# A mixture-of-experts layer whose gathered token blocks are transposed on VectorE instead of TensorE

## What is computed

```python
def swiglu(t, wg, wu, wd):
    return (jax.nn.silu(t @ wg) * (t @ wu)) @ wd

def moe_ffn(h, ...):                       # h: 512 x 1024
    scores = jax.nn.sigmoid(t @ w_router)  # 64 experts, group-limited top 8
    ...
    wts = wts / jnp.sum(wts, axis=-1, keepdims=True) * ROUTED_SCALE
    ...
    def expert_block(args):
        tok, wb, e = args
        xb = t_pad[tok]                    # gather the rows of this block
        yb = swiglu(xb, w_e_gate[e], w_e_up[e], w_e_down[e])
        return yb * wb[:, None]
    ...
    routed = jax.ops.segment_sum(yb.reshape(P, d), slot_tok, num_segments=T + 1)[:T]
    shared = swiglu(t, w_sh_gate, w_sh_up, w_sh_down)
    return routed + shared
```

## Time and profile before

| What | us |
|---|---|
| Median of three runs (lowest, highest) | 1122.77 (1122.42, 1122.96) |
| The profiled execution, whole | 1125.14 |
| Its span in the trace | 1123.3 |
| First gate_up of the loop starts | 402.82 |
| Last gate_up of the loop starts | 1083.4 |
| TensorE busy (share of the span) | 1030.9 (92%) |
| VectorE busy | 442.9 (39%) |
| ScalarE busy | 437.9 (39%) |
| GpSimd busy | 371.0 (33%) |

### The profile page before, as it was taken

How to read it: one execution, slowest core, us unless ns; L and a number is a source line. 1 busy time by engine, 2 the same in 40 slices (tenths; PEclk the granted TensorE clock), 3 DMA queues, 4 the chain that set the end, 5 groups by cost and what they waited for, 6 DMA issues and landing times.

```text
span 1123.3 us, 20142 instructions
## 1 busy us (share of the span) xinstructions
PE 1030.9 (92%) x6035; PEld 543.3 (48%) x6036; DVE 442.9 (39%) x727; ACT 437.9 (39%) x929; POOL 371.0 (33%) x242
## 2 busy tenths in 40 slices
PE   1899999899999999899999799999999999999980
PEld 0554443566455644455455355455555554554540
DVE  0445776874478522222232223232232232322325
ACT  3312122575343534334444334444444434444442
POOL 1112233000000044344444335454444444444440
PEclk9999999999999999999999999999999999999995
DMA  9933255700007389999759999999988986999915
GB/s 311 391 138 143 92 207 183 295 1 1 19 38 280 137 318 387 402 385 374 226 163 343 402 390 388 297 388 335 398 283 256 350 312 199 369 386 361 321 14 224
DMA packets 76169, 295.10 MB, mean 263 GB/s; under 512 B 16657, under 2 KB 17169, under 8 KB 56433
## 3 DMA queue, kind: packets, MB, share of 16 engines
q1 hardware_dynamic: 50386, 258.01, 58.2%
q0 software_dynamic: 24336, 34.29, 13.8%
q10 hardware_dynamic: 1424, 2.52, 0.6%
HBM read 280.83 MB, written 36.44 MB: 282 GB/s over the span
## 4 chain that ended last, share of the span: by engine, by line
PE 71%; DMA 13%; DVE 6%; issue 3%; ACT 3%; POOL 2%; SPq 1%; DVEq 0%; ACTq 0%; POOLq 0%
PE psum L1104 32%; PE psum L1113 16%; PE psum L1091 5%; DMA wring<-in_w_e_down 4%; DMA ring<-in_w_ada 4%; DMA heads<-in_w_ada 3%; PE psum L912 2%; PE psum L1120 2%; PE psum L1063 2%; PE psum L934 2%; PE psum L880 2%; PE psum L963 2%; PE psum L943 2%; POOL ring L488 2%; DVE heads L1242 1%
## 5 line engine op out<-in xcount | busy, mean ns | idle before, releaser
L1104 PE MATMUL psum<-wring,rows 128*64 x1664 | 387.2, 386 | 15.5 <-issue 14.3
L1104 PE MATMUL psum<-cur_g,rows 128*64 128x256 f32 x1664 | 387.5, 387 | 0.0
L1104 PEld LDWEIGHTS psum<-wring,rows 128*64 128x64 f32 x1664 | 222.0, 138 | 136.4 <-issue 31.5
L504 POOL DMA_INDIRECT expert_sums<-rows,sidx x107 | 203.9, 1906 | 96.0 <-issue 73.7
L1104 PEld LDWEIGHTS psum<-cur_g,rows 128*64 128x64 f32 x1664 | 222.0, 138 | 0.0
L498 POOL DMA_INDIRECT xg<-h_rows,gidx x107 | 114.0, 1065 | 291.4 <-ACT gidx L739 281.8
L1113 PE MATMUL psum<-wring,rows 128*64 x420 | 202.7, 605 | 1.6 <-issue 1.6
L1113 PE MATMUL psum<-cur_d,rows 128*64 128x512 f32 x420 | 202.7, 605 | 0.0
L1504 DVE COPY cur_g<-wring 128x2048 f32 x105 | 128.8, 1227 | 127.2 <-issue 86.2
L736 ACT COPY cur_d<-wring 128x1024 f32 x105 | 109.8, 1046 | 29.2 <-issue 29.2
L800 ACT COPY rows<-psum 128x512 f32<-128x512 f32 x105 | 61.5, 585 | 133.0 <-PE psum L1113 125.8
(11 more groups left out here) (223 smaller groups left out, 998.4 us busy)
## 6 DMA issues: line engine op xcount, KB each, us to landing
wring<-in_w_e_gate SPq DMA_DIRECT2D x64, 1024.0 KB
wring<-in_w_e_up SPq DMA_DIRECT2D x64, 1024.0 KB
wring<-in_w_e_down SPq DMA_DIRECT2D x64, 1024.0 KB
ring<-in_w_ada SPq DMA_DIRECT2D x16, 1024.0 KB, 4.8
ring<-in_w_in SPq DMA_DIRECT2D x4, 2048.0 KB, 29.8
ring<-in_w_ada SPq DMA_DIRECT2D x2, 2048.0 KB, 24.8
heads<-in_w_ada SPq DMA_DIRECT2D x2, 2048.0 KB, 33.4
ring<-in_w_out SPq DMA_DIRECT2D x1, 4096.0 KB, 16.4
```

Source lines behind the costliest of these rows:

```text
L504: pool.indirect_dma_start(srows[q], bass.IndirectOffsetOnAxis(sidx[:, q:q + 1].bitcast(U32), 0), ysb[:, q, :], None, bounds_check=2 * T - ...
L1104: last = pe.matmul(pp[2][SUB * g:SUB * g + SUB, 512 * q:512 * q + 2 * P] .rearrange("p (u f) -> p u f", u=2), xT[:, q, k % 4, c0:c0 + SUB] ...
```

## The change

`h` is stored in its natural order, and `gather` fetches quarters: partition 32*c + r of `xg` gets the 256 features of quarter c of the tokens in slots r (first half of the free dimension) and 32 + r (second half). That takes two indirect DMAs a block, of 128 rows of 1 KB each, where there was one of 128 rows of 2 KB. Since a quarter is what 32 partitions of the weights hold (eight features each), transposing each 32x32 piece within its 32 partitions gives `xT`. VectorE does this in one operation (`turn_block` in its own list, behind `copy_gate_up` and ahead of `hmid`), with a read stride of eight floats. TensorE's `turn_block` and ScalarE's `evacuate_block` are gone. `gather_index` copies two columns and waits until VectorE has turned the block whose buffer it frees.

The indices need each slot's token on four groups of partitions. TensorE gets eight small matmuls for it (`quarters`) in the middle of the last shared gate_up, between VectorE's copy of the raw table and VectorE's operations that make the indices. `expert_input` reads without a stride; `turn_h` takes every eighth column instead.

The core of the diff:

```diff
             def gather(b, q, set_by):
                 pool.wait_ge(s_gi, set_by)
                 pool.sem_inc(s_pgo, 1)
-                pool.indirect_dma_start(xg[:, q, :], None, hrows, bass.IndirectOffsetOnAxis(gidx[:, q:q + 1].bitcast(U32), 0),
-                                        bounds_check=2 * T - 1, oob_is_err=False).then_inc(s_gt[q], 16)
+                for s in range(2):
+                    pool.indirect_dma_start(xg[:, q, 256 * s:256 * s + 256], None, hrows,
+                                            bass.IndirectOffsetOnAxis(gidx[:, q, s:s + 1].bitcast(U32), 0),
+                                            bounds_check=4 * T - 1, oob_is_err=False).then_inc(s_gt[q], 16)
...
-            def evacuate_block(n, q):
-                act.wait_ge(s_xt, n)
-                act.copy(xT[:, q], pp[1][:, 512 * q:512 * q + 512].rearrange("p (k s) -> p k s", k=4)).then_inc(s_xte, 1)
...
             def gather_index(b, q):
-                act.copy(gidx[:, q:q + 1], slot_idx[:, bass.ds(b + 1, 1)]).then_inc(s_gi, 1)
+                act.wait_ge(s_xte, b - 1)
+                act.copy(gidx[:, q, :], slot_g[:, bass.ds((b + 1) * 2, 2)]).then_inc(s_gi, 1)
...
                 for k in range(KD):
-                    last = pe.transpose(pp[3][:, k * P:(k + 1) * P], y1[:, t % 2, k * P:(k + 1) * P], ident)
+                    last = pe.transpose(pp[3][:, k * P:(k + 1) * P],
+                                        y1[:, t % 2, k:D:KD], ident)
...
+            def quarters():
+                pe.wait_ge(s_raw, 1)
+                for s in range(2):
+                    for c in range(4):
+                        last = pe.matmul(pp[2][32 * c:32 * c + 32, MAXB * s:MAXB * s + MAXB],
+                                         cst[:, C_ID + 32 * s:C_ID + 32 * s + 32], vraw, start=True, stop=True)
+                last.then_inc(s_sel2, 1)
...
-                    c0 = SUB * (k // 4)
...
-                                         xT[:, q, k % 4, c0:c0 + SUB], cur_g[:, q, :, k, :] if g else w[:, :, k, 0:P],
+                                         xT[:, q, k, :], cur_g[:, q, :, k, :] if g else w[:, :, k, 0:P],
...
-            shared_gate_up(3, range(4, KD))
+            shared_gate_up(3, range(4, 6))
+            quarters()
+            shared_gate_up(3, range(6, KD))
             shared_down(2)
             shared_hidden(3)
+            shared_down(3)
             pe.wait_ge(s_clr, 2)
-            pe.wait_ge(s_gt[0], 16)
-            turn_block(0)
-            shared_down(3)
...
                     gate_up(q, w0)
-                    pe.wait_ge(s_gt[1 - q], i * 8 + 16 * (q + 1))
-                    turn_block(1 - q)
...
+            def turn_block(q, gathered):
+                dve.wait_ge(s_gt[q], gathered)
+                dve.transpose(xT[:, q].rearrange("p k (s r) -> p s k r", s=2),
+                              xg[:, q, :].rearrange("p (s r k) -> p s k r", s=2, k=KD)).then_inc(s_xte, 1)
...
                     copy_gate_up(i + (q + 1), 1 - q)
+                    turn_block(1 - q, i * 16 + 32 * (q + 1))
                     dve.wait_ge(s_sil, i + (q + NT + 1))
```

More of the change, by code:

```diff
@@ L68 @@
 C_EPS = C_FAC + 64
-NCONST = C_EPS + 1
+C_QUART = C_EPS + 1
+NCONST = C_QUART + 1
 def constants():
@@ L100, in constants @@
     c[:, C_EPS] = EPS
+    c[:, C_QUART] = 2 * FAR + p // 32
     return c, rope
@@ L120, in build @@
         slot_idx = sb("slot_idx", [P, 136], I32)
-        gidx = sb("gidx", [P, 2], I32)
+        gidx = sb("gidx", [P, 2, 2], I32)
         sidx = sb("sidx", [P, 2], I32)
@@ L215, in build @@
         weq = heads[:, 3072:5120].rearrange("p (c k e) -> p c k e", c=NT, k=TOPK)
-        xT = rows[:, 0:1024].rearrange("p (b k q) -> p b k q", b=2, k=4)
+        slot_g = cst[:, C_TRI:C_TRI + 2 * 136].bitcast(I32)
+        vraw = rows[:, 1024:1024 + MAXB]
+        xT = rows[:, 0:1024].rearrange("p (b k q) -> p b k q", b=2, k=KD)
         ysb = rows[:, 1024:2048].rearrange("p (b n) -> p b n", b=2)
@@ L336, in build @@
         s_gt = [sem(f"gathered{i}") for i in range(2)]
-        s_xt = sem("block_transposed")
-        s_xte = sem("block_evacuated")
+        s_xte = sem("block_transposed")
+        s_raw = sem("slot_tokens_kept")
+        s_sel2 = sem("slot_tokens_by_quarter")
         s_gu = sem("gate_up")
@@ L490, in _ @@
             pool.memset(zeros, 0.0).then_inc(s_zero, 1)
-            hrows = hbuf.rearrange("t (h n) -> (t h) n", h=2)
+            hrows = hbuf.rearrange("t (h n) -> (t h) n", h=4)
             srows = [x.rearrange("t (h n) -> (t h) n", h=2) for x in sums]
@@ L541, in _ @@
             pool.wait_ge(s_scat[1], n_odd)
-            pool.wait_ge(s_gt[0], n_odd)
-            pool.wait_ge(s_gt[1], n_even)
+            n_g0 = pool.snap(pairs * 32 + 64)
+            n_g1 = pool.snap(pairs * 32 + 32)
+            pool.wait_ge(s_gt[0], n_g0)
+            pool.wait_ge(s_gt[1], n_g1)
             pool.sem_inc(s_routed, 1)
@@ L787, in _ @@
             shared_keep(3)
-            evacuate_block(1, 0)
             shared_rows(3)
-            act.wait_ge(s_idx, 1)
+            act.wait_ge(s_idx, 2)
             gather_index(2, 0)
@@ L805, in _ @@
                     act.activation(sg, pp[2][:, 512 * q:512 * q + P], ACT.Silu).then_inc(s_sil, 1)
-                    evacuate_block(i + (q + 2), 1 - q)
                     gather_index(i + (q + 3), 1 - q)
@@ L1087, in shared_down @@
                 last.then_inc(s_dn, 1)
[L1089 to L1093, removed]
             def weights_of(b):
@@ L1379, in expert_input @@
                 then(dve.reciprocal(hrst[:, t:t + 1], hrst[:, t:t + 1]))
[L1380 to L1385, removed]
+                h = y1[:, t % 2, :]
+                then(dve.scalar_tensor_tensor(h, xres[:, t, :], hrst[:, t:t + 1], arow[:, 2], ALU.mult, ALU.mult))
+                dve.tensor_tensor(h, h, arow[:, 1], ALU.add).then_inc(s_h, 1)
             score_maxima(0)
@@ L1493, in _ @@
             dve.wait_ge(s_tm, NT)
-            dve.tensor_scalar(gidx[:], pp[3][:, 0:2], cst[:, C_HALF:C_HALF + 1], None, ALU.add).then_inc(s_gi, 1)
-            then(dve.tensor_scalar(slot_idx[:, 1:1 + MAXB], pp[3][:, 0:MAXB], cst[:, C_HALF:C_HALF + 1], None, ALU.add))
+            dve.tensor_copy(vraw, pp[3][:, 0:MAXB]).then_inc(s_raw, 1)
+            dve.tensor_scalar(slot_idx[:, 1:1 + MAXB], pp[3][:, 0:MAXB], cst[:, C_HALF:C_HALF + 1], None, ALU.add)
             then(dve.tensor_copy(slot_w[:, 0:MAXB], pp[3][:, MAXB:2 * MAXB]))
+            dve.sem_inc(s_idx, 1)
+            dve.wait_ge(s_sel2, 1)
+            tok = pp[2][:, 0:2 * MAXB].rearrange("p (s b) -> p b s", s=2)
+            dve.tensor_scalar(gidx[:], tok[:, 0:2, :], 2.0, cst[:, C_QUART:C_QUART + 1], ALU.mult, ALU.add)\
+               .then_inc(s_gi, 1)
+            dve.tensor_scalar(slot_g[:, 2 + 2 * MAXB:2 * 136], vraw[:, 0:14], 0.0, 4 * FAR, ALU.mult, ALU.add)
+            then(dve.tensor_scalar(slot_g[:, 2:2 + 2 * MAXB].rearrange("p (b s) -> p b s", s=2), tok, 2.0,
+                                   cst[:, C_QUART:C_QUART + 1], ALU.mult, ALU.add))
             dve.sem_inc(s_idx, 1)
@@ L1504, in copy_gate_up @@
                 dve.tensor_copy(cur_g[:, q], w[:, :, :, P:]).then_inc(s_cgu, 1)
+            def turn_block(q, gathered):
+                dve.wait_ge(s_gt[q], gathered)
+                dve.transpose(xT[:, q].rearrange("p k (s r) -> p s k r", s=2),
+                              xg[:, q, :].rearrange("p (s r k) -> p s k r", s=2, k=KD)).then_inc(s_xte, 1)
             copy_gate_up(0, 0)
             shared_mid(3)
+            dve.wait_ge(s_clr, 1)
+            turn_block(0, 32)
             nb = dve.value_load(ntab[0:1, 0:1], min_val=E, max_val=MAXB - 1)
```

## The result

The changed kernel takes 1127.67 us (median of 9 runs, 1124.62 to 1132.41), the kernel before 1122.84 (9 runs, 1121.66 to 1124.59). The ratio is 1.0045 with a 95% interval of 1.0029 to 1.0061. The forecast was 1091 us, with a range of 1075 to 1111. The profiled run of the changed kernel took 1129.58 for a span of 1126.6, 3.3 longer than the span before.

What follows compares the result with a forecast made beforehand. The prediction took TensorE's queue to bound the loop, with weight loads close behind. Loop -34, before the loop +1 and clock +1 gave -32 us from 1122.8, so 1091 us, range 1075 to 1111.

Steps and rivals of the forecast that it cites:

- TensorE waits for nobody: Expert loop: hmid is ready 1.57 us before turn_hidden needs it, so work leaving TensorE's queue shortens the 6.44 us step.
- TensorE's transposes: Expert loop, between gate_up and down: removing the block transposes saves 0.58 us a step (0.50 to 0.64), 60 us over 104.
- VectorE's transpose: Expert loop, between copy_gate_up and hmid: takes 1.12 us (0.73 to 2.25), hidden behind the wait for silu.
- Rival D: VectorE's transpose in the loop is far slower and delays hmid; at 4 us the kernel takes 1159; chance 0.04.
- GpSimd: Expert loop: two gather issues and a scatter take 4.95 us a step, under 5.86, so it does not bound.
- Rival C: GpSimd sets the loop's pace, 6.18 us a step when VectorE's copy holds a second issue; 1110 us; chance 0.10.
- When the rows land: Expert loop: the second gather lands at 13.1, TensorE feels it only from 15.4; margin 2.3 us, no cost.
- Rival B: Quartered gathers land late, so VectorE's transpose, hmid and turn_hidden wait in the loop; 1180 us; chance 0.09.
- Before the loop: Prologue: a VectorE copy and eight small matmuls delay the first gather, partly covered by shared_down(3); net +1 us (-1 to +2).
- What the DMA takes back: Expert loop: weight loads limit half the steps; 52 steps gain 30 us, the other 52 gain 4; loop -34 us.
- The clock: TensorE restarts slowly after long waits (granted clock 0.94 against 1.00); +1 us for what the DMA does not hide.
- The forecast's own bounds: Whole kernel: 1078 (0.64 a step, other half 0.44) to 1102 us (0.50 a step, other half 0, prologue +2).

## Why the prediction was wrong

**TensorE waits for nobody.** This is the step that failed: "TensorE waits for nobody: hmid, which turn_hidden needs, was ready at 804.44 + 0.35 = 804.79, 1.57 us early. So what leaves TensorE's queue shortens the step, until something else is late." I compared hmid's end with the start of turn_hidden, where it did have 1.57 us to spare, and took that for the slack of the whole chain. The chain goes on: two reads, 804.84 to 806.31 in that step, stand between hmid and gate_up. The two kinds of step have to be laid side by side. In the steps of 6.42 gate_up came 1.93 behind hmid in both kernels (medians of the steps shorter than 7.3 us), so there was nothing to spare; in those of 6.32 it came 1.84 behind hmid, and 1.82 in the changed kernel, 0.02 to spare. The step that I had read, of 6.44, was itself one that the sequencer set: gate_up follows turn_hidden there by 0.38, where TensorE's queue alone takes 0.26. The trace of before had it all: the program's order puts `weights_of` behind the wait for hmid, and the view of its line has 209 reads with a median of 0.303 us for the load alone. I had costed TensorE's matmuls but not the sequencer that issues them. The Trainium skill (Perfetto Trace Analysis, "Sequencer Loop") says that a sequencer pushes engine instructions into a queue and executes control instructions itself. The traces agree: the reads have records of their own on the sequencer. The same page ("Tensor Engine Instruction (MATMUL, LD_WEIGHTS)") has the sequencer ready for the next instruction once it has pushed a matmul or weight load that waits for its semaphore. The measurement differs: the wait for hmid is that of turn_hidden's weight load, and in 102 of the 104 steps of before the sequencer's next record starts 0.05 us after hmid's end, after up to 1.8 us without one. So the reads behind turn_hidden did not start before hmid was done, though turn_hidden itself ran only at 806.36.

**TensorE's transposes: 0.58 a step.** Right in kind, a little small: TensorE's own step goes from 6.32 to 5.58, 0.74, for down follows gate_up by 0.21 and not 0.32, and its first record is shorter as well. It counts only with the reads moved: the changed kernel as it stands has steps of 6.28 and 6.41.

**VectorE's transpose: 1.12 us.** It took 1.10 (1.085 to 1.120), and idled only 14.2 us ahead of it. Hmid was still released by silu in most steps. Rival D is out.

**GpSimd.** A gather's issue takes 1.20 in the mean, 1.75 where it runs into VectorE's copy (803.44 and 803.84 in the step above). By the prediction's sum a step takes it 2 x 1.20 + 1.88 + 3 x 0.30 = 5.18. It is busy 510.8 us of the span, but it waits for the index 99 times (171.4 us), and in the kernel with steps of 5.58 still 45 times (100.5 us). Rival C is out.

**When the rows land.** They came in time in the changed kernel: VectorE waited for them 3 times, 7.8 us. Rival B is out. In the shorter step it waits 29 times, 22 us, so the margin of 2.3 us was no margin of every step.

**Before the loop: +1 (-1 to +2).** The first gate_up started at 402.82 before and at 405.08 after. In the profiled runs of the three kernels with TensorE's transposes it was at 401.5 to 403.0, mean 402.4; in the eleven with VectorE's at 401.3 to 405.8, mean 404.0. The difference is +1.6. With +1.4 in the loop it makes most of the 3.3 us in span; no run takes the two apart from the spread between runs, so why it came out slower and not equal is argued, not shown.

**What the DMA takes back.** I took 26 of 60. With the reads moved in both kernels TensorE's work falls by 103 x 0.74 = 76 us and the sum of the steps by 668.8 - 635.6 = 33.2, so 43 are taken back, most of it probably by the loads (34.3 us came back with a sixth less to load). The forecast of -34 for the loop agrees with this 33.2 partly by luck: the work that left was larger than I took, and so was what came back.

**The clock: +1.** The mean granted clock of the profiled runs is 0.981 before, 0.979 in the changed kernel and 0.971 with the reads moved. No run shows what that costs.

**The odds.** The forecast's own bounds were also added up wrong: 52 x 0.64 + 52 x 0.44 = 56 us off, with +1 and +1, gives 1069 and not 1078, and 52 x 0.50 = 26 off, with +2 and +1, gives 1100 and not 1102. So the range left out the fast end of the forecast itself; rivals B and D, the slower ones, make 0.13 and not 0.11. Neither touches the miss. None of the five rivals was this one, and 0.04 for "same" and 0.11 for "slower" stood on mechanisms that did not occur. All five asked what the new work would cost. None asked whether the old work had been on the path at all.

## What to carry to other kernels

Before an instruction's time is counted as a gain, find the chain that ends at the next one in program order on the same engine, control work included: a wait, register reads and address arithmetic behind it, and only then the matmul. If the timeline leaves that work out, look at the view of its source line. Read values for the next step before the wait that ends last, not behind it; a step that looks full (TensorE busy 99%) can stand 0.02 us from being bound by its sequencer, or be bound by it every second time. And to see what a removed operation was worth, put it back once with the suspected cover and once without.

## What was not expected of the hardware

A read of one table entry into a register of TensorE's sequencer, with the address arithmetic behind it, costs about 0.7 us (0.46, 1.16, 1.82 and 2.66 us for 0, 1, 2 and 3 reads), more than a transpose of a 128x128 block there (0.33) and about as much as the four that the change removed. Of this the load's record is 0.30 and the arithmetic's 0.20; the rest lies between records. The timeline shows it only as idle time "issue" ahead of the next matmul, the view of the source line shows the records. The sequencer held at the wait of turn_hidden's weight load, and its next record came 0.05 us after hmid's end. Ahead of the wait, while TensorE works off gate_up and down, two such reads leave no gap in its step.
